# K's projection as pairs of 64-row half-array matmuls, with its two partial sums joined outside TensorE

## What is computed

```python
h = rms_norm(x, mix_norm_g[layer])
proj = h @ w_in[layer]                       # (256, 1024) @ (1024, 2560)
xr, yg, q, k, v = jnp.split(proj, splits, axis=-1)          # each 512 wide
xr = causal_depthwise_conv(xr, lru_conv_w[layer], lru_conv_b[layer])
y_lru = rg_lru(xr, ...) * jax.nn.gelu(yg)
q = rms_norm(q.reshape(bsz, seq, ATTN_HEADS, HEAD_DIM), q_norm_g[layer])
k = rms_norm(k.reshape(bsz, seq, ATTN_HEADS, HEAD_DIM), k_norm_g[layer])
y_attn = moba_attention(q, k, v)             # 256 tokens: causal attention, 8 heads of 64
x = x + jnp.concatenate([rms_norm(y_lru, ...), rms_norm(y_attn, ...)]) @ w_out[layer]
hf = rms_norm(x, ffn_norm_g[layer])          # then the FFN: w_up, conv, gelu(gate) * val, w_down
```

## Time and profile before

| | |
|---|---|
| three runs, median (lowest to highest) | 292.11 us (292.09 to 292.11) |
| profiled execution, span from its first to its last instruction | 290.4 us |
| outside the span, by the median | 1.7 us |
| TensorE busy | 285.6 us (98%) |
| VectorE busy | 243.9 us (84%) |
| ScalarE busy | 202.6 us (70%) |
| share of TensorE in the chain that ended last | 95% |
| K's products, 20.48 to 31.36 us | 10.88 us |

### The profile page before, as it was taken

The page is one execution under the profiler, slowest core; times in us unless marked ns, Lnnn a source line. Parts: engine busy times, 40 slices in busy tenths (PEclk is TensorE's granted clock), DMA queues, the critical chain, the costliest instruction groups (busy, mean ns, idle before and its releaser), DMA issues.

```text
span 290.4 us, 5009 instructions
## 1 busy us (share of the span) xinstructions
PE 285.6 (98%) x1646; PEld 247.3 (85%) x1646; DVE 243.9 (84%) x447; ACT 202.6 (70%) x381; POOL 11.9 (4%) x28
## 2 busy tenths in 40 slices
PE   7999999999999999999999999999999999999996
PEld 7688999898788998888888888888888888888885
DVE  2998898889999778999888888888888888888865
ACT  4793599999884689777766666667676666676540
POOL 4000005500000000000000000000000000000000
PEclk9999999999999999999999999999999999999999
DMA  7999950441274704475637464454747344200003
GB/s 281 423 422 419 389 184 0 147 144 26 121 271 165 266 25 147 144 289 164 272 146 290 147 217 176 161 179 147 278 144 288 146 169 168 96 0 0 0 0 144
DMA packets 8111, 52.23 MB, mean 180 GB/s; under 512 B 928, under 2 KB 1312, under 8 KB 2080
## 3 DMA queue, kind: packets, MB, share of 16 engines
q1 hardware_dynamic: 7920, 51.50, 47.7%
q0 software_dynamic: 176, 0.53, 0.5%
HBM read 50.98 MB, written 1.05 MB: 179 GB/s over the span
## 4 chain that ended last, share of the span: by engine, by line
PE 95%; DMA 2%; DVE 1%; ACT 1%; SPq 0%; issue 0%
PE bank L1385 26%; PE bank L1044 15%; PE bank L1045 14%; PE bank L1048 14%; PE bank L1389 14%; PE bank L1100 3%; DMA x_tok<-in_x_dram 2%; PE bank L1352 1%; PE bank L1360 1%; PE bank L1164 1%; PE bank L1288 1%; PE bank L1195 1%; PE bank L1204 1%; PE bank L1322 1%; PE bank L1158 1%; DVE w_hi L678 0%
## 5 line engine op out<-in xcount | busy, mean ns | idle before, releaser
L688 DVE TENSOR_TENSOR w_lo<-raw,w_hi 128x1024 fp32r<-128x1024 f32 x94 | 112.1, 1221 | 5.6 <-ACT w_hi L376 5.0
L376 ACT ACTIVATE w_hi<-raw 128x1024 fp32r<-128x1024 f32 x85 | 86.4, 1059 | 3.5 <-PE bank L1048 3.1
L1385 PE MATMUL bank<-h_both,w_hi 128*128 128x512 f32 x336 | 83.7, 391 | 0.0
L1385 PEld LDWEIGHTS bank<-h_both,w_hi 128*128 128x128 f32 x336 | 61.6, 188 | 11.8
L1389 PEld LDWEIGHTS bank<-h_both,w_lo 128*128 128x128 f32 x336 | 45.8, 190 | 3.3
L1389 PE MATMUL bank<-h_both,w_lo 128*128 128x256 f32 x336 | 46.8, 282 | 0.0
L603 ACT ACTIVATE tanh_a<-bank 128x256 f32<-128x256 f32 x44 | 16.8, 382 | 40.3 <-PE bank L1389 40.1
L1045 PE MATMUL bank<-w_lo,act_hi 128*128 128x512 f32 (+1 forms) x90 | 34.8, 387 | 0.0
L1044 PE MATMUL bank<-w_hi,act_hi 128*128 128x512 f32 (+1 forms) x90 | 34.8, 387 | 0.0
L1048 PE MATMUL bank<-w_hi,act_lo 128*128 128x512 f32 (+1 forms) x90 | 34.6, 384 | 0.0
L611 ACT ACTIVATE xc<-ygate,par 128x256 f32<-128x256 f32 x44 | 26.2, 595 | 3.6 <-DVE ygate L969 3.6
(11 more groups left out here) (186 smaller groups left out, 397.6 us busy)
## 6 DMA issues: line engine op xcount, KB each, us to landing
raw<-in_stream_dram SPq DMA_DIRECT2D x47, 1024.0 KB, 4.9
x_tok<-in_x_dram SPq DMA_DIRECT2D x2, 512.0 KB, 5.0
out_dram<-x_tok SPq DMA_DIRECT2D x3, 256.0 KB, 2.0
p_T<-in_gates_dram POOLq DMA_DIRECT2D x1, 512.0 KB, 9.5
out_dram<-x_tok SPq DMA_DIRECT2D x2, 128.0 KB, 2.0
par<-in_params_dram SPq DMA_DIRECT2D x1, 117.0 KB, 6.6
mix_g<-in_params_dram POOLq DMA_DIRECT2D x1, 4.0 KB, 5.6
```

The source lines that it names most:

```text
L376: act.activation(w_hi[u % RING][:, :], raw_unit(u), ACT.Copy).then_inc(hi_done, 1)
L688: dve.tensor_tensor(w_lo[u % RING][:, :], raw_unit(u), w_hi[u % RING][:, :].bitcast(F32), ALU.subtract).then_inc(lo_done, 1)
L1385: pe.matmul(acc[:, :], whi[:, kc, :], h_both[:, kc, :, :].rearrange("p b t -> p (b t)"), start=kc == 0, stop=False)
```

## The change

K's 128-row matmuls become pairs of 64-row matmuls: for every chunk, part and token tile, one matmul contracts the array rows 0 to 63 into banks 2 and 3 (`K_ACC`), and the next one the rows 64 to 127 into banks 6 and 7 (`K_LOWER`). Each streams 512 columns. That makes 96 matmuls and 96 weight loads in place of 48 and 48. All of a chunk's matmuls now wait for `lo` of its unit, also the first four. K is then the sum of two banks: ScalarE copies banks 6 and 7 to SBUF (`k_copy`), VectorE adds banks 2 and 3 to the copies (`k_add`, into `k_raw`, a part of `p_T` that is free then), ScalarE squares `k_raw` (`k_squares`), and the norm reads `k_raw` in place of the banks. TensorE waits for `k_copied` before X's unit 10, whose bank is 6.

```diff
+        K_LOWER = bank[6:8]
+        k_raw = [flat(p_T)[:, 512 * m:512 * (m + 1)] for m in range(TT)]
...
+            def k_copy(m):
+                act.wait_ge(unit_used, U_X)
+                act.activation(k_raw[m], K_LOWER[m][:, :], ACT.Copy).then_inc(k_copied, 1)
+
+            def k_squares(m):
+                act.wait_ge(k_added, m + 1)
+                act.wait_ge(qk_sum, TT + m)
+                act.activation(sq_tok, k_raw[m], ACT.Square).then_inc(qk_sq, 1)
...
-            squares(2, K_ACC[0], U_X - 1)
-            squares(3, K_ACC[1], U_X - 1)
+            k_copy(0)
+            k_copy(1)
+            k_squares(0)
+            k_squares(1)
             roots(2)
...
+            def k_add(m):
+                dve.wait_ge(unit_used, U_X)
+                dve.wait_ge(k_copied, m + 1)
+                dve.tensor_tensor(k_raw[m], K_ACC[m][:, :], k_raw[m], ALU.add).then_inc(k_added, 1)
...
             los(9, 10, 11)
+            k_add(0)
+            k_add(1)
             head_sums(2)
             head_sums(3)
-            head_norms(2, K_ACC)
+            dve.wait_ge(k_added, TT)
+            head_norms(2, k_raw)
...
-            for j in range(1, 4):
-                rows_unit(U_K + j, U_K, K_ACC)
+            def k_half(kc, m, part, rows):
+
+                u, cols, tok = U_K + kc // 2, slice(512 * (kc % 2), 512 * (kc % 2 + 1)), slice(P * m, P * (m + 1))
+                lhs, rhs = ((h_hi, w_hi), (h_hi, w_lo), (h_lo, w_hi))[part]
+                acc = (K_ACC if rows.start == 0 else K_LOWER)[m]
+                return pe.matmul(acc[:, :], lhs[rows, kc, tok], rhs[u % RING][rows, cols],
+                                 start=kc == 0 and part == 0, stop=kc == KC - 1 and part == 2)
+
+            for kc in range(KC):
+                split(U_K + kc // 2)
+                for part in range(3):
+                    for m in range(TT):
+                        k_half(kc, m, part, slice(0, HALF))
+                        ins = k_half(kc, m, part, slice(HALF, P))
+                if kc % 2:
+                    ins.then_inc(unit_used, 1)
             cols_unit(U_X, X_ACC[0][:, 0:SEQ])
             cols_unit(U_X + 1, X_ACC[1][:, 0:SEQ])
             pe.wait_ge(qk_norm, 2 * TT)
             for c in range(LC):
                 transpose_qk(c)
+            pe.wait_ge(k_copied, TT)
             cols_unit(U_X + 2, X_ACC[2][:, 0:SEQ])
```

More of the change, by code:

```diff
@@ L211, in build_layer @@
         qkT, qkT_read = sem("qkT"), sem("qkT_read")
+        k_copied, k_added = sem("k_copied"), sem("k_added")
         v_half, v_ready = sem("v_half"), sem("v_ready")
@@ L444, in squares @@
                     act.wait_ge(qk_sum, g)
-                act.activation(sq_tok, acc[:, :], ACT.Square).then_inc(qk_sq, 1)
+                act.activation(sq_tok, acc, ACT.Square).then_inc(qk_sq, 1)
+            def k_copy(m):
[5 more added lines that the diff above has]
+                act.activation(sq_tok, k_raw[m], ACT.Square).then_inc(qk_sq, 1)
             def roots(g):
@@ L470, in p_out @@
                 act.activation(p_T[:, h, :], P_BANK[h % 4][:, 0:SCORES], ACT.Copy).then_inc(pT_read, 1)
-            squares(0, Q_ACC[0], U_K - 1)
-            squares(1, Q_ACC[1], U_K - 1)
+            squares(0, Q_ACC[0][:, :], U_K - 1)
+            squares(1, Q_ACC[1][:, :], U_K - 1)
             roots(0)
             his(9, 10, 11)
-            squares(2, K_ACC[0], U_X - 1)
-            squares(3, K_ACC[1], U_X - 1)
+            k_copy(0)
+            k_copy(1)
+            k_squares(0)
+            k_squares(1)
             roots(2)
@@ L762, in head_norms @@
                     dve.tensor_tensor(qk_tok[:, g + m, :].rearrange("p (h d) -> p h d", h=HEADS),
-                                      acc[m][:, :].rearrange("p (h d) -> p h d", h=HEADS),
+                                      acc[m].rearrange("p (h d) -> p h d", h=HEADS),
                                       qk_rstd[:, g + m, :].unsqueeze(2).to_broadcast([P, HEADS, HEAD_DIM]),
@@ L803, in _ @@
             head_sums(1)
-            head_norms(0, Q_ACC)
+            head_norms(0, [acc[:, :] for acc in Q_ACC])
             los(9, 10, 11)
+            k_add(0)
+            k_add(1)
             head_sums(2)
             head_sums(3)
-            head_norms(2, K_ACC)
+            dve.wait_ge(k_added, TT)
+            head_norms(2, k_raw)
             los(12, 13)
```

## The result

The changed kernel takes 293.01 us (median of 7 runs, 292.78 to 293.11); the kernel before, run beside it, 292.11 (7 runs, 291.78 to 292.20). The ratio is 1.0034, with a 95% interval from 1.0024 to 1.0044: 0.99 us slower, between 0.70 and 1.29. The forecast was 293.0, range 292.4 to 293.7. The profiled execution has a span of 291.4 us against 290.4.

What follows compares the result with a forecast made beforehand. TensorE's own stream was taken to bound the kernel. The norm's 1.62 us less 0.87 slack, plus 0.05 and 0.06, gave 0.86, with 0.39 for switches inside it; 292.11 + 0.86 = 292.97, forecast 293.0 us, range 292.4 to 293.7.

Steps and rivals of the forecast that it cites:

- the slack of 0.87 us: Between the end of K's norm at 36.24 and TensorE's transposes at 37.11; all that covers a longer norm.
- The pairs' step: In K's products, a pair of 64-row matmuls runs side by side in 0.2267 us, so K changes by 0.
- B: Rival: K's pairs have the short step, -0.51 us on K; +0.35 in all, 292.46 us, chance 0.24.
- C: Rival: each half pays its own overhead, 0.240 us a step, +0.64 on K; 293.6 us, chance 0.13.
- E: Rival: K's fp32r pairs don't run side by side, +10.9 us on K; 303.9 us, chance 0.03.
- The wait for unit 4's low part: Ahead of K: costs nothing, as the low part is done at 20.18 and K begins at 20.48.
- The switches: Going to half-array matmuls at K's start and back at its end: +0.39 us on TensorE, bounds 0.2 to 0.5.
- The norm: Behind K, entry, copy and addition make the norm end 1.62 us later than 36.24.
- At the transposes: TensorE 0.86 us later: 1.62 less 0.87 slack, plus 0.05 wake-up and 0.06 exposed load; bounds 0.39 to 1.1.
- What is late next: Gates, attention and output projection: latenesses 0.58, 0.55 and 0.81 us, none over TensorE's 0.86, so nothing added.
- D: Rival: the join costs less than its rows because hand-overs overlap; about +0.45, 292.6 us, chance 0.07.
- the 0.05: Chance for the part of the forecast's own spread, 0.4 to 1.1 us, that lies under 0.58.

Runs made afterwards that it cites:

- e8: The kernel before with one superfluous ScalarE copy of K's bank 2 ahead of K's first square; 292.07 us against 292.05, ratio 1.0001.
- e7: The changed kernel without the join and with only K's lower-half matmuls, 48 of 64 rows; 292.43 us against 292.01, ratio 1.0015.
- e2: The changed kernel with its join kept but K's matmuls 48 full-array ones again; 292.88 us against 292.05, ratio 1.0029.
- e1: The changed kernel with its pairs but no join: no copies or additions, norm reads banks 2 and 3 alone; 292.44 us against 292.05, ratio 1.0013.
- e3: The changed kernel with K's even chunks as half-array pairs, odd chunks as full-array matmuls, eight switches; 294.59 us against 292.01, ratio 1.0086.
- e4: The changed kernel with token tile 0's products before tile 1's in K's last unit, tile 0 joined early; 292.54 us against 292.05, ratio 1.0020.
- e10: As e4, with two double waits of VectorE made single; 292.68 us against 292.02, ratio 1.0024.
- e9: The changed kernel with two double waits of VectorE made single, one wait moved to the first head sum; 293.03 us against 292.02, ratio 1.0034.
- e6: The changed kernel with halves alternating by twos: lower for both token tiles, then upper for both; 293.10 us against 292.01, ratio 1.0040.

## Why the prediction was right, point by point

- **What bounds the kernel, and the slack of 0.87 us.** Right. e8 uses 0.49 of it for nothing. Beyond that the cost is the norm's lateness less 0.78, which is the slack, 0.88 by the ns, less the wake-up and the exposed load, within 0.01.
- **The pairs' step: taken as 0.2267, bounds 0.216 and 0.240.** Right: 0.2277 with its slow start, 0.2267 in the steady stream. The choice of the row of the same type and rate over the half-array row of the other type decided it. The argument that the small overhead goes with the half-rate stream and not with half of the array is shown by e7. Rivals B and C fall by this number, E by the two starts side by side.
- **The rule of the Trainium skill on weight loads and row groups.** The Trainium skill ("TensorE: Matmul & The Clock Gate", Part 3 (The mechanism)) lets a weight load overlap with matmuls in flight only when its row group differs. The runs do not bear that out: the loads of the full-array matmuls and of e7's, always on the same rows, are hidden, and the pairs, which alternate row groups, have the same step of 0.2267. The 292.5 of rival B, with a shorter step, did not come.
- **The wait for unit 4's low part: nothing.** Right in the changed kernel, by e2. The margin is thin: in e1's profile the low part came 0.18 later and K's first pair 0.03. The copies ahead of X's unit 10 end at 32.86, 6.9 us before it starts at 39.80 and not some 5; nothing hangs on that.
- **The switches: +0.39 for two.** The size is a little off: 0.45 (e1) or 0.41 (e7) for two, 0.225 each where they follow closely (e3). The rows at the scores gave the gap and the first step rightly (0.20 and 0.19 there, 0.20 and 0.195 here); what they do not show is that the next steps of 512 columns are some 0.005 longer for a while. The 0.43 by which TensorE's stream is later at the end of X is about 0.20 + 0.19 for the switches and 0.05 for these steps.
- **The norm: +1.62.** Measured +1.82. The mis-sized pieces are 0.05 of the slow steps ahead of K's end, 0.06 for two squares that take 0.63 from SBUF and not 0.60 as from PSUM, and 0.14 for two hand-overs that became 0.10 because the late one of their two semaphores is waited for by a separate instruction; the hand-over from the addition to the first square was 0.06 shorter than costed, because there it is not. I had taken every hand-over from the place in the old order, and not from which of the semaphores comes last.
- **At the transposes: +0.86.** Measured: the second transpose starts 1.055 later, made up of the norm's 1.82 less 0.88 of slack, plus 0.055 wake-up and 0.06 exposed load. The last two terms were right.
- **What is late next: nothing.** Right. The stretch as a whole is 1.045 longer and the transposes 1.055; nothing was added or given back in the 250 us behind them. I had ScalarE's queue 1.2 late there. At the transposed Q it was (39.04 against 37.81), but at the output projection VectorE and TensorE are equally late, and the margin is the old 0.39.
- **The sum.** 0.86 against 1.05 in the trace and 0.99 (0.70 to 1.29) by the ratio. The mechanism was right at each step; all mis-sized terms but one hand-over were on the low side, 0.19 in all. That the forecast of 292.97 lies 0.04 from the median of 293.01 is luck: single runs of the changed kernel differ by up to 0.33.
- **The chances.** By its own list B, D and the 0.05 make 0.36 for a time within 0.2%; less the 0.02 kept for a gain that is 0.34 and not the 0.33 written; nothing hangs on it.
- **Rival D**, a join that costs less than its rows: it costs more. A version that hides it (e4, e10) is still slower than the kernel before, since TensorE's own 0.45 stays. No version here beats the kernel before.

## What to carry to other kernels

Splitting a matmul that used all 128 rows buys two switches and a sum of two banks for the same step time. By e7 and e1 the second half of a pair costs TensorE nothing, so pairs should pay where a matmul would otherwise leave half of the rows unused; no run here has that case. A join that is off TensorE's path costs its length less the slack of what it precedes, so look first at how long the consumer can wait, and order the last products so that one tile is complete early, with the engine that joins it free at that time. Where an instruction waits for two semaphores, look which of them comes last and whether that one is waited for by a separate instruction (here the wait written last); cost the hand-over by that, not by the neighbour's gap.

## What the runs showed of the hardware beyond that

- In these kernels, of two semaphores before an instruction of VectorE or ScalarE, the one written last is waited for by an instruction of its own. If that is the late one, the hand-over is 0.09 to 0.10 us in place of 0.03 (addition, reciprocal, e9's first sum, second square); if the other is late, it stays 0.03 (first square).
- A stream of 512-column fp32r matmuls runs its first eight or so steps behind a switch (changed kernel, e3, e7) at 0.224 to 0.241 us, mostly 0.23, before they settle at 0.2267. e2 has the same at K's start without a switch or a gap. The cause is open.
- 64-row fp32r matmuls that all use the same rows (e7) have hidden weight loads and the full-array step, 0.2267 us.
- Half-array matmuls need not alternate strictly to run side by side: ordered by twos (e6) they took the same time to 0.01 us.
- A square of 128 x 512 on ScalarE, in K's norm, takes 0.63 us from SBUF and 0.60 from PSUM.
